# A two-block network on one core: the convolution's channel sums on GpSimd, the memory's squares on ScalarE with VectorE adding them, hgrn heads written out

## What is computed

```python
v = depthwise_conv31(a * sigmoid(b)) + dw_b         # 2048 channels
v = silu(layer_norm(v, ln_g, ln_b))                 # mean and variance over the channels
x = x + (v * silu(z)) @ w_out
x = x + hgrn2_mixer(rms_norm(x))                    # 16 heads
h = rms_norm(x, g_mix) @ w_in                       # k, v of NSA, compressed over 32 tokens by w_ck1, w_cv1
hm = rms_norm(mem, g_mem)                           # the memory, used later by w_ck and w_cv
x = x + attend(rms_norm(x), hm) @ w_co              # cross attention
hf = rms_norm(x, g_ffn); x = x + (silu(hf @ w_g) * (hf @ w_u)) @ w_down
```

## Time and profile before

| what | us |
|---|---|
| median of 3 runs | 2381.38 (2381.38 to 2383.58) |
| the profiled execution, its own time | 2375.67 |
| its span, first to last instruction | 2373.9 |
| TensorE busy (matmuls) | 2299.2, 97% |
| VectorE busy | 1677.7, 71% |
| ScalarE busy | 1270.2, 54% |
| GpSimd busy | 255.2, 11% |

### The profile page before, as it was taken

How to read it: one execution, slowest core, us unless ns; L and a number is a source line. 1 busy time by engine, 2 the same in 40 slices (tenths; PEclk the granted TensorE clock), 3 DMA queues, 4 the chain that set the end, 5 groups by cost and what they waited for, 6 DMA issues and landing times.

```text
span 2373.9 us, 37625 instructions
## 1 busy us (share of the span) xinstructions
PE 2299.2 (97%) x14114; PEld 2045.4 (86%) x14114; DVE 1677.7 (71%) x2541; ACT 1270.2 (54%) x1435; POOL 255.2 (11%) x66
## 2 busy tenths in 40 slices
PE   6999999999999999989999988998999999999999
PEld 6999988888888888877888877887888888888888
DVE  6777776778878787777676766757666566655666
ACT  6565565666666666445666656465433343333443
POOL 4777730000000000030000000001000000000000
PEclk9999999999999999999999999999999999999999
DMA  6444444444444443556444422534455555555556
GB/s 227 169 173 177 178 178 177 176 158 164 158 161 159 160 159 127 209 196 231 162 157 145 157 89 98 185 125 160 178 193 180 192 185 186 192 180 194 185 197 219
DMA packets 57419, 409.25 MB, mean 172 GB/s; under 512 B 6496, under 2 KB 6624, under 8 KB 8544
## 3 DMA queue, kind: packets, MB, share of 16 engines
q1 hardware_dynamic: 57312, 407.84, 47.6%
HBM read 405.71 MB, written 2.10 MB: 172 GB/s over the span
## 4 chain that ended last, share of the span: by engine, by line
PE 89%; DVE 5%; ACT 3%; issue 1%; DMA 1%; SPq 0%; DVEq 0%; ACTq 0%
PE G L351 23%; PE G L350 23%; PE G L349 12%; PE G L352 12%; PE G L358 4%; PE G L359 4%; PE G L360 4%; DMA RAW<-stream_dram 1%; ACT HI L327 1%; DVE LO L334 1%; PE A L1013 1%; PE A L1040 1%; PE A L1001 1%; DVE HXB L2388 0%; PE A L1015 0%
## 5 line engine op out<-in xcount | busy, mean ns | idle before, releaser
L327 ACT ACTIVATE HI<-RAW 128x2048 fp32r<-128x2048 f32 x381 | 727.8, 1912 | 775.7 <-DMA RAW<-stream_dram 774.6
L334 DVE TENSOR_TENSOR LO<-RAW,HI 128x2048 fp32r<-128x2048 f32 x332 | 762.1, 2297 | 150.2 <-ACT HI L327 139.5
L351 PE MATMUL G<-HX,HI 128*128 128x512 f32 x1544 | 621.1, 402 | 4.8 <-DVE HX L493 2.6
L350 PE MATMUL G<-HX,HI 128*128 128x512 f32 x1544 | 612.2, 397 | 0.0
L349 PE MATMUL G<-HX,LO 128*128 128x256 f32 x1544 | 435.5, 282 | 0.0
L352 PE MATMUL G<-HX,LO 128*128 128x256 f32 x1544 | 434.4, 281 | 0.0
L351 PE MATMUL G<-HXB,HI 128*128 128x512 f32 x992 | 391.6, 395 | 11.0 <-DVE HXB L2388 8.8
L350 PE MATMUL G<-HXB,HI 128*128 128x512 f32 x992 | 393.8, 397 | 0.0
L349 PEld LDWEIGHTS G<-HX,LO 128*128 128x128 f32 x1544 | 290.5, 188 | 67.5
L352 PEld LDWEIGHTS G<-HX,LO 128*128 128x128 f32 x1544 | 291.8, 189 | 61.3
L351 PEld LDWEIGHTS G<-HX,HI 128*128 128x128 f32 x1544 | 295.9, 192 | 10.7 <-DVE LO L334 3.3
(11 more groups left out here) (367 smaller groups left out, 2626.4 us busy)
## 6 DMA issues: line engine op xcount, KB each, us to landing
RAW<-stream_dram SPq DMA_DIRECT2D x381, 1024.0 KB, 4.8
X<-x_dram SPq DMA_DIRECT2D x4, 512.0 KB, 5.4
MB<-mem_dram SPq DMA_DIRECT2D x4, 512.0 KB, 7.0
out_dram<-X SPq DMA_DIRECT2D x4, 512.0 KB, 7.7
CON<-constants_dram SPq DMA_DIRECT2D x1, 996.0 KB, 15.9
VEC<-vectors_dram SPq DMA_DIRECT2D x1, 623.5 KB, 16.9
VEC<-vectors_dram SPq DMA_DIRECT2D x1, 272.0 KB, 6.8
CON<-constants_dram SPq DMA_DIRECT2D x1, 64.5 KB, 1.9
```

The lines of the kernel that those rows point to most:

```text
L327: nc.scalar.activation(HI[:, c.slot(RING), :], RAW[:, c.slot(RING), :], ACT.Copy).then_inc(hi_ready, 1)
L334: nc.vector.tensor_tensor(LO[:, c.slot(RING), :], RAW[:, c.slot(RING), :], HI[:, c.slot(RING), :].bitcast(F32), ALU.subtract).then_inc(lo_ ...
L350: return nc.tensor.matmul(res, wh, both[:, k, :, :], start=False, stop=last)
L351: nc.tensor.matmul(res, wh, both[:, k, :, :], start=first, stop=False)
```

## The change

- Convolution: GpSimd adds CV and SC of tiles 0 to 13 into two tiles CS and CQ (the two halves of the buffer SQ), each pair of adds behind one of its splits. TensorE multiplies ones with CS and CQ once, then with tiles 14 and 15.
- hgrn: on TensorE, ScalarE and VectorE all 16 heads are written out.
- Mixer A: ScalarE squares the memory, in four instructions behind its work in vc1, K0, ks1 and vs0; VectorE adds, behind ks0, ks1 and vs0. The sum on TensorE stands after vs1, the roots at V0, the scaling of MB in pairs behind kw0, V1, kw1, V2, and four each behind vw0 and vw1. The table for Silu is loaded at kw0. GpSimd has no work there.
- Cross attention: sums_x runs once for each group, with four matmuls, and the plan lets the first product start with eight tiles. GpSimd has no work there. The split of chunk C_CO + 2 stands before exps(2) on ScalarE, and on VectorE before rest(2).

```diff
         SUMS = 3
+        POOL_SUMS = KT - 2
...
-                    project(ft, 0, sums(ft - 2))
+                    project(ft, 0)
...
         def conv_sums(pe, ft):
-            f = ft.v if isinstance(ft.v, int) else 1
+            last = ft.v == KT - 1
+            if not last:
+                pe.wait_ge(cv_sums, POOL_SUMS)
+                nc.tensor.matmul(A[4][:, 0:T], ONES, CS, start=True, stop=False, skip_group_check=True)
+                nc.tensor.matmul(A[5][:, 0:T], ONES, CQ, start=True, stop=False, skip_group_check=True)
             wait(pe, cv_done, ft + 1)
-            nc.tensor.matmul(A[4][:, 0:T], ONES, tile(CV, ft), start=(f == 0), stop=(f == KT - 1), skip_group_check=True)
+            nc.tensor.matmul(A[4][:, 0:T], ONES, tile(CV, ft), start=False, stop=last, skip_group_check=True)
             wait(pe, cv_sq, ft + 1)
-            nc.tensor.matmul(A[5][:, 0:T], ONES, SC[:, ft.slot(2), :], start=(f == 0), stop=(f == KT - 1),
+            nc.tensor.matmul(A[5][:, 0:T], ONES, SC[:, ft.slot(2), :], start=False, stop=last,
                              skip_group_check=True).then_inc(cv_sums, 1)
...
         def conv_pool(pool):
+            def add(ft):
+                pool.wait_ge(cv_done, ft + 1)
+                wait(pool, cv_sums, ft)
+                if ft:
+                    nc.gpsimd.tensor_tensor(CS, CS, CV[:, ft, :], ALU.add)
+                else:
+                    nc.gpsimd.tensor_copy(CS, CV[:, ft, :])
+                pool.wait_ge(cv_sq, ft + 1)
+                if ft:
+                    nc.gpsimd.tensor_tensor(CQ, CQ, SC[:, ft % 2, :], ALU.add).then_inc(cv_sums, 1)
+                else:
+                    nc.gpsimd.tensor_copy(CQ, SC[:, ft % 2, :]).then_inc(cv_sums, 1)
+            added = {conv_chunk(ft + 2, 0).v + 3: ft for ft in range(POOL_SUMS)}
             for p in range(2, C_CONVO + 3):
                 split_lo_pool(pool, At(p))
+                if p in added:
+                    add(added[p])
...
-            for j in range(4):
+            for j in range(HEADS):
                 head(At(j), At(j - 1) if j else None)
-            with pe.Fori(1, 4) as i:
-                for j in range(4):
-                    head(At(j, 4, i), At(j - 1, 4, i))
...
-        MEM_SUM_AFTER = "ks1"
+        squares_after, adds_after = ["vc1", "K0", "ks1", "vs0"], ["ks0", "ks1", "vs0"]
+        scaled_after = ["kw0", "V1", "kw1", "V2", "vw0", "vw0", "vw1", "vw1"]
...
-                if name == MEM_SUM_AFTER:
-                    pe.wait_ge(n_sq, norm_mem.sq(KT))
+                if name == "vs1":
+                    pe.wait_ge(mx_ms, 5)
                     nc.tensor.matmul(A[5][:, 0:T], ONES, HN[:, 0, 0, :], start=True, stop=True).then_inc(n_ss, KT)
...
+                if name == "kw0":
+                    act.preload_act_table_set("silu_and_others")
                 if name == "kc1":
                     windows(0)
-                if name == "K2":
+                if name == squares_after[0]:
+                    act.wait_ge(s_mem, 64)
+                if name in squares_after:
+                    g = squares_after.index(name)
+                    if g > 1:
+                        act.wait_ge(mx_ms, g - 1)
+                    nc.scalar.activation(HN[:, min(g, 1)], MB[:, g * GRP:(g + 1) * GRP, :], ACT.Square).then_inc(n_sq, GRP)
+                if name == "V0":
                     act.wait_ge(n_ss, norm_mem.sq(KT))
...
-            pool.wait_ge(s_mem, 64)
-            squares(0, sums)
-            for g in range(1, KT // GRP):
-                pool.wait_ge(pool_sum, 2 * g - 1)
-                squares(g, more)
-                pool.wait_ge(pool_sum, 2 * g)
-                nc.gpsimd.tensor_tensor(sums, sums, more, ALU.add).then_inc(pool_sum, 1)
-            pool.wait_ge(pool_sum, 7)
-            nc.gpsimd.tensor_tensor(HN[:, 0, 0:2], HN[:, 0, 0:2], HN[:, 0, 2:4], ALU.add).then_inc(pool_sum, 1)
-            pool.wait_ge(pool_sum, 8)
-            pool.wait_ge(n_ss, norm_mem.sq(0))
-            nc.gpsimd.tensor_tensor(HN[:, 0, 0], HN[:, 0, 0], HN[:, 0, 1], ALU.add).then_inc(n_sq, KT)
...
-                if name in ("V0", "kw0", "V1", "kw1"):
-                    g = ("V0", "kw0", "V1", "kw1").index(name)
-                    dve.wait_ge(mx_mr, 2)
-                    for k in range(g * GRP, (g + 1) * GRP):
-                        ins = nc.vector.scalar_tensor_tensor(MB[:, k, :], MB[:, k, :], vec("g_mem", k), RM[:], ALU.mult, ALU.mult)
-                    ins.then_inc(n_hn, 1)
+                if name in adds_after:
+                    g = adds_after.index(name) + 1
+                    dve.wait_ge(n_sq, norm_mem.sq(GRP * (g + 1)))
+                    if g > 1:
+                        dve.wait_ge(mx_ms, g - 1)
+                    nc.vector.tensor_tensor(HN[:, 0], HN[:, 0], HN[:, 1], ALU.add).then_inc(mx_ms, 1)
+                    if g == 3:
+                        for n2 in (2, 1):
+                            dve.wait_ge(mx_ms, 5 - n2)
+                            nc.vector.tensor_tensor(HN[:, 0, 0:n2], HN[:, 0, 0:n2], HN[:, 0, n2:2 * n2], ALU.add).then_inc(mx_ms, 1)
+                for two in range(8):
+                    if scaled_after[two] == name:
+                        dve.wait_ge(mx_mr, 2)
+                        for k in (2 * two, 2 * two + 1):
+                            ins = nc.vector.scalar_tensor_tensor(MB[:, k, :], MB[:, k, :], vec("g_mem", k), RM[:], ALU.mult, ALU.mult)
+                        if two % 2:
+                            ins.then_inc(n_hn, 1)
...
-            def sums_x(pe):
-                res = A[norm_ff.bank][:, 0:T]
-                pe.wait_ge(pool_sum, 12)
-                nc.tensor.matmul(res, ONES, HN[:, 0, 0, :], start=True, stop=False)
-                pe.wait_ge(n_sq, norm_ff.sq(KT))
+            def sums_x(g):
+                pe.wait_ge(n_sq, norm_ff.sq(GRP * (g + 1)))
                 for k in range(GRP):
-                    mm = nc.tensor.matmul(res, ONES, HN[:, 1, k, :], start=False, stop=(k == GRP - 1))
-                mm.then_inc(n_ss, KT)
+                    nc.tensor.matmul(A[norm_ff.bank][:, 0:T], ONES, HN[:, g % 2, k, :], start=(g == 0 and k == 0),
+                                     stop=(g * GRP + k == KT - 1), skip_group_check=True).then_inc(n_ss, 1)
...
             output(2, 0, 4)
+            sums_x(0)
             pe.wait_ge(cr_x, 4)
             output(3, 0, 4)
-            parts[0].plan = [(0, 0, 12), sums_x, (1, 0, 8), (0, 12, 16), (1, 8, 16)]
+            sums_x(1)
+            parts[0].plan = [(0, 0, 8), lambda pe: sums_x(2), (0, 8, 12), (1, 0, 4), lambda pe: sums_x(3), (1, 4, 8), (0, 12, 16), (1, 8, 16)]
...
+            split_hi(act, At(C_CO + 2))
             exps(2)
             exps(3)
             turned(2)
             high(2)
             turned(3)
             high(3)
-            split_hi(act, At(C_CO + 2))
...
-                wait(act, pool_sum, 7 + cc if cc > 1 else 0)
-                nc.scalar.activation(HN[:, min(cc, 1)], X[:, GRP * cc:GRP * (cc + 1), :], ACT.Square).then_inc(n_sq, GRP)
+                wait(act, n_ss, norm_ff.sq(GRP * (cc - 1)) if cc > 1 else 0)
+                nc.scalar.activation(HN[:, cc % 2], X[:, GRP * cc:GRP * (cc + 1), :], ACT.Square).then_inc(n_sq, GRP)
...
-            for g in (1, 2):
-                pool.wait_ge(n_sq, norm_ff.sq(GRP * (g + 1)))
-                pool.wait_ge(pool_sum, 7 + g)
-                nc.gpsimd.tensor_tensor(HN[:, 0], HN[:, 0], HN[:, 1], ALU.add).then_inc(pool_sum, 1)
...
+            split_lo(dve, At(C_CO + 2))
             rest(2)
             rest(3)
+            split_lo(dve, At(C_CO + 3))
...
-            split_lo(dve, At(C_CO + 2))
-            split_lo(dve, At(C_CO + 3))
```

34 lines of the change are left out of this document (7 added, 27 removed).

## The result

The changed kernel takes 2348.44 us (median of 4 executions, 2347.61 to 2349.41) against 2381.38 us for the kernel before in the same session (2379.63 to 2383.58): ratio 0.9861, 95% interval 0.9844 to 0.9878. It is faster by 1.4%, and the forecast of 2352 us was 3.6 us too high. The profiled execution took 2347.61 us, 28.06 less than the profiled one of before. The difference of the medians, 32.9, is larger, because the three runs shown with the kernel before lay 5.7 us above its profile. 54 further executions of it, taken beside the experiments, have their median at 2377.5, only 1.8 above the profile.

What follows compares the result with a forecast made beforehand. TensorE, busy for 97% of the span, was taken to bound the kernel. 11.2 (convolution) + 0 (hgrn) + 11.1 (mixer A) + 7.0 (cross attention to feed-forward) = 29.3 us, so 2381.38 - 29.3 = 2352 us, range 2342 to 2366.

Steps and rivals of the forecast that it cites:

- The convolution, 11.2 us: Convolution: 13 pairs of sums fewer on TensorE, at 0.86 us each, would save 11.2 us.
- GpSimd hides an add up to 1.66 us: Convolution: GpSimd's added work stays covered by TensorE's products as long as each add takes under 1.66 us.
- GpSimd holds the convolution: Rival, convolution: adds costing 2 us instead of 0.74 keep the stage at its present pace; total 2363, chance 0.07.
- hgrn, 0: hgrn heads: writing them out gains nothing, since heads 3 and 4 both end 32.85 us after the one before.
- rival "slower": Rival, heads 4 to 15: written-out heads, some 700 TensorE instructions each, outrun instruction supply; 2388 at 3 us a head, chance 0.02.
- Mixer A, 11.1 us: Mixer A: with GpSimd silent VectorE runs alone; 11.1 us gained, 6.8 + 2.3 by K1 and 2.0 behind it.
- K0 starts 6.8 us sooner: Mixer A: K0 would start 6.8 us sooner than 1056.98, behind vc1, and the clock would stay up.
- where I had 9.1: Mixer A: K1 would start at 1061.1 instead of 1070.16, 9.1 us sooner, its 3.3 us gap staying.
- the 1.88 us of L1419: Mixer A: TensorE's 1.88 us wait before L1419 would go, with HS ready when V1 ends.
- a stall moved: Rival, mixer A: the gap before K1 lowers the clock or ScalarE is late; mixer gives 7, total 2359, chance 0.17.
- Cross attention to feed-forward, 7.0 us: Cross attention to feed-forward: the first pair of products ends 7.1 us sooner, taken as 7.0, bounds 4 and 7.5.
- above all the product no longer needs 12 tiles to start: Start of feed-forward: the main reason given for the gain, said to be what the 8.81 us wait was.

Runs made afterwards that it cites:

- e13_hgrn_only: The kernel before with all 16 hgrn heads written out and nothing else changed: 2376.51 us, ratio 1.0003.
- e1_conv_only: The kernel before with only the change's convolution part, hgrn heads still looped: 2375.67 us, ratio 0.9993.
- e4_hgrn_loops: The changed kernel with hgrn heads 4 to 15 put back into a loop of three turns: 2358.73 us.
- e3_mix_and_cross: The kernel before with only the mixer A and cross-attention parts of the change: 2360.03 us, ratio 0.9923.
- e5_pool_later: The kernel before, its memory squares kept on GpSimd but started after VectorE's mixer windows, with what hangs on their sum moved behind: 2373.93 us, ratio 0.9986.
- e7_plan12: The changed kernel with the first feed-forward product again starting with 12 tiles instead of eight: 2348.31 us.
- e10: The changed kernel with two further GpSimd adds into unused tiles ahead of every sum add of the convolution: 2366.07 us.

## Why the prediction was right, step by step

**The convolution, 11.2 us.** Right in size (11.2 by the table) and in reason. The claim that GpSimd hides an add up to 1.66 us was tested beyond its edge and gave 14.1 us against 14.6. The rival "GpSimd holds the convolution" needed adds of 2 us; they take 0.74.

**hgrn, 0.** Right for the step taken alone (e13_hgrn_only) and right for the sum, but incomplete, and by a lot. I read from the earlier trace rows that entering the loop costs nothing and took it as a property of the loop. It is a property of where the loop lies in that one program. The convolution part shifts it, and the jumps then cost 7.7 us (e1_conv_only) to 9.9 us (e4_hgrn_loops). Had the change come without the written-out heads, my sum of 29.3 would have been 10 us off, and nothing in my text would have said why. The forecast held because the change had both pieces, which is luck: I had no reason for the pair. I had cited the Trainium skill ("Runtime: NRT & Kernel Launch", Instruction fetch mechanics) for taken branches that stall until their target is fetched; the page says this of a target outside the two pages that it takes to be loaded, a condition that I left out. The top of this loop is some 1,700 instructions away, far outside two pages of 256. By that rule, the trace agrees in kernels where the loop does not stay loaded (about 3.9 us a jump) and disagrees in the kernel before (nothing). I also looked at heads 3 and 4 only: those show the way into the loop, not a jump back. The rows that bear on it are those behind heads 7 and 11. The 700 instructions a head of my rival "slower" were wrong too: four written-out heads are 1,672, so a head is 418, and the supply kept up with it.

**Mixer A, 11.1 us.** Measured 9.7 in the change and 10.3 in e3_mix_and_cross. The reason, VectorE slowed by GpSimd beside it, is shown by e5_pool_later. All of the following are net of the 10.8 us that the stage begins sooner. K0 starts 6.8 us sooner (1039.45 against 1056.98), as worked out, and is through 8.3 us sooner, since the clock stays up: my text named the clock, but that 1.5 was in no term of my sum. K1 starts 9.5 us sooner, where I had 9.1, with its gap as forecast. The terms that failed come behind it. The clock fell at K1 and ks1, and that is a matter of the execution. In e7_plan12, with the same code and the same wait of 2.83 us before K1, it did not fall:

```profile
1049.00:1051.00 2.00, 1.57 (x14) 1.31 (x12) 2.00 (x1) 2.00 (x2) 0.00 (x0) 1.00 0.47 197
1051.00:1053.00 2.00, 1.77 (x10) 1.57 (x11) 1.97 (x4) 1.49 (x1) 0.00 (x0) 1.00 0.49 111
```

Counted from mixer A's first product, the two profiles of this mixer without the fall (e7 and e10) gain 11.0 us each and the three with it (the change, e3, e4) 9.7 to 10.4. So the 11.1 are met where the clock stays up, and up to 1.3 us of the shortfall are the clock. The other term is the 1.88 us of L1419, which I had go; 1.09 stayed, because HS stands behind a split whose transfer came late, three table loads and two more splits (ScalarE's timeline):

```profile
1075.46 1.92 ACT L328 ACTIVATE HI<-RAW 128x2048 fp32r<-128x2048 f32 x1 [1.52 <-DMA RAW<-stream_dram]
...
1084.27 1.91 ACT L328 ACTIVATE HI<-RAW 128x2048 fp32r<-128x2048 f32 x1
1086.09 0.20 ACT L1502 ACTIVATE HS<-A 128x60 f32<-128x60 f32 x1
```

That the sum still comes to 11.0 without the fall is in part luck: 0.4 us more than forecast by K1 stand against 0.5 less behind it. It is the rival "a stall moved" in small: its gap and, in three of five profiles, its clock fall are there, its 4 us are not.

**Cross attention to feed-forward, 7.0 us.** Measured 7.0. But "above all the product no longer needs 12 tiles to start" was wrong as to what mattered: e7_plan12 needs twelve and loses nothing. With the low parts back at 1.69 us and the splits out of their way, the third set is there in time.

**The median.** The sum of 29.3 against 28.1 found between the two profiles is 1.2 too much, all of it in mixer A, which gave 1.4 less than forecast. The forecast took the offset of 5.7 us between the three runs and the profile as given and came out 3.6 high. With a median of 2377.5 from 54 executions the same sum gives 2348.2. How long an execution of this kernel takes goes with its clock: those 54, grouped by mean granted clock, have means of 2380.9 us at 0.989 (one), 2378.4 at 0.990, 2377.4 at 0.991, 2376.5 at 0.992 and 2374.0 at 0.993. The change runs at 0.993 to 0.995, with a spread of 1.8 us. (A 55th execution of the kernel before took 4575.72 us, for no reason that I know, and is left out.)

## What to carry to other kernels

Before you cost an edit at "so many instructions less", ask what else lies behind them in the same engine's program: a loop that stays loaded may stop doing so when its place shifts, and the price shows as idle time with no releaser right behind the loop's last instruction, far from the edit. Count the instruction packets over the loop in the DMA view of both kernels; if they are many more, pad the place back or write the loop out. And when two engines slow each other, put the work on a third or run it apart, but check in the other's rows that the time does not come back one stage on; when two edits cure the same stall, test each alone before you credit one.

## What the runs showed of the hardware

- A loop of about 131 us of TensorE work (four heads) runs its second and third turn with no packet of queue 8 in one place of the program, and with one every 20 us in another. In the second case each jump back costs 3.8 to 4.0 us, with up to 1.9 more where the clock falls behind it. 
- VectorE and GpSimd slow each other: a 128x256 scaling 0.43 us alone and 1.88 or 2.06 beside GpSimd, a 128x2048 split 2.29 alone and 4.1 to 4.5 beside it, GpSimd's 128x1024 add 2.5 to 2.7 us beside the windows and 4.3 beside two of three splits. Yet GpSimd's splits and adds in the convolution leave VectorE's 128x256 taps, with one input in PSUM, at 482 to 484 ns, with 26 adds more or 78 more, while one 128x256 product of two SBUF inputs took 4.58 us beside a GpSimd split instead of 0.42.
- An f32 matmul of only 64 columns, with its weight load, took the tensor engine some 0.43 us at the start of the program (26 of them held it from 5.43 to 16.6 us), so idle matmuls are no free padding.
- A clock fall needs no long stop, and the same stop does not always bring one: 2.82 us of idle time before K1 were followed by 0.50 in the change, 2.83 us at the same place of the same code in e7_plan12 were not, nor were 2.88 in the kernel before.
